# Moving a free unit of work inside the hosted groups of a fused attention and convolution block

## What is computed

```
h    = rmsnorm(concat(meta, x)) * gain                       # 272 x 2048
q, k, v, f, z_att, u, gate_b, gate_c, z_conv, m_att, m_conv = split(h @ w_in)
y_att  = (forgetting_attention(q, k, v, log_sigmoid(f + b_f)) * silu(z_att)) @ w_att_o
y_conv = (gate_b * short_conv(gate_c * u, conv_w) * silu(z_conv)) @ w_conv_o
out  = rmsnorm(x + (sigmoid(m_att) * y_att + sigmoid(m_conv) * y_conv) @ w_out) * final_gain
```

## Time and profile before

| what | value |
| --- | --- |
| median of 3 runs | 1211.78 us (1211.6 to 1213.21) |
| profiled execution, own time | 1212.1 us |
| its span, first to last instruction | 1210.4 us |
| granted TensorE clock, mean | 0.997 |
| TensorE busy | 1198.9 us, 99% |
| VectorE busy | 954.3 us, 79% |
| ScalarE busy | 651.3 us, 54% |
| the six hosted groups | 62.9 to 604.2 us of the span |

### The profile page before, as it was taken

One profiled execution on the slowest core, in us unless ns is written; L12 is line 12 of the kernel. 1 busy time (PEld: TensorE's weight loads), 2 busy tenths in 40 slices (PEclk: granted clock), 3 DMA queues, 4 the chain that ended last, 5 costly groups with the idle time before them and its releaser, 6 DMA issues.

```text
span 1210.4 us, 18441 instructions
## 1 busy us (share of the span) xinstructions
PE 1198.9 (99%) x7252; PEld 1070.5 (88%) x7252; DVE 954.3 (79%) x1111; ACT 651.3 (54%) x868; POOL 35.3 (3%) x50
## 2 busy tenths in 40 slices
PE   8999999999999999999999999999999999999997
PEld 8998898898888988889888899999999999888886
DVE  6989989989989989989966546877787778755544
ACT  7566556556556556656555444445544554543533
POOL 1000000000000000000000010111011101000000
PEclk9999999999999999999999999999999999999999
DMA  6798898897888898898678865555755565665663
GB/s 214 245 301 270 277 296 257 279 304 251 277 288 290 265 300 272 267 310 267 193 237 260 275 184 179 154 170 164 209 154 171 152 204 165 224 205 181 210 218 129
DMA packets 181249, 280.40 MB, mean 232 GB/s; under 512 B 9296, under 2 KB 128160, under 8 KB 180768
## 3 DMA queue, kind: packets, MB, share of 16 engines
q1 hardware_dynamic: 171760, 263.49, 68.1%
q10 hardware_dynamic: 9408, 15.78, 4.1%
HBM read 270.83 MB, written 8.41 MB: 231 GB/s over the span
## 4 chain that ended last, share of the span: by engine, by line
PE 89%; DVE 8%; issue 1%; ACT 1%; DMA 1%; ACTq 0%; POOLq 0%; POOL 0%; DVEq 0%
PE ps L1480 22%; PE ps L1482 22%; PE ps L1481 22%; PE ps L1494 13%; PE ps L1495 7%; DVE w_lo L1052 2%; DVE w_lo L1089 1%; DVE w_lo L1086 1%; DVE quads L1068 1%; DVE quads L1070 1%; DVE quads L1066 1%; DMA chan_rows<-in_norm_gain 1%; PE ps L1503 0%; PE ps L1527 0%; PE ps L1678 0%
## 5 line engine op out<-in xcount | busy, mean ns | idle before, releaser
L934 DVE TENSOR_TENSOR w_lo<-w_raw,w_hi 128x1024 fp32r<-128x1024 f32 x196 | 237.8, 1232 | 98.5 <-ACT w_hi L610 97.8
L1480 PE MATMUL ps<-h,w_hi 128*128 128x258 f32 (+1 forms) x1024 | 293.6, 287 | 1.2 <-DVE w_lo L1052 0.9
L1481 PE MATMUL ps<-h,w_hi 128*128 128x258 f32 (+1 forms) x1024 | 291.2, 284 | 0.0
L1482 PE MATMUL ps<-h,w_lo 128*128 128x258 f32 (+1 forms) x1024 | 290.9, 284 | 0.0
L1494 PE MATMUL ps<-h,w_hi 128*128 128x512 f32 x768 | 273.5, 398 | 0.3 <-DVE w_lo L1052 0.3
L610 ACT CAST w_hi<-w_raw 128x1024 fp32r<-128x1024 f32 x198 | 203.4, 1050 | 112.5 <-PE ps L1482 68.2
L1495 PE MATMUL ps<-h,w_lo 128*128 128x256 f32 x768 | 215.2, 280 | 0.0
L1480 PEld LDWEIGHTS ps<-h,w_hi 128*128 128x128 f32 x1024 | 192.7, 188 | 5.3 <-issue 1.8
L1481 PEld LDWEIGHTS ps<-h,w_hi 128*128 128x128 f32 x1024 | 192.9, 188 | 1.8
L1482 PEld LDWEIGHTS ps<-h,w_lo 128*128 128x128 f32 x1024 | 192.8, 188 | 0.0
L1494 PEld LDWEIGHTS ps<-h,w_hi 128*128 128x128 f32 x768 | 144.3, 188 | 35.8 <-DVE w_lo L1052 1.0
(11 more groups left out here) (209 smaller groups left out, 1836.3 us busy)
## 6 DMA issues: line engine op xcount, KB each, us to landing
w_raw<-in_w_in SPq DMA_DIRECT2D x226, 512.0 KB, 4.8
quads<-in_w_in SPq DMA_DIRECT2D x144, 512.0 KB, 4.5
w_raw<-in_w_conv_o SPq DMA_DIRECT2D x32, 512.0 KB, 5.9
w_raw<-in_w_att_o SPq DMA_DIRECT2D x32, 512.0 KB, 4.6
w_raw<-in_w_out SPq DMA_DIRECT2D x32, 512.0 KB, 4.7
quads<-in_w_in SPq DMA_DIRECT2D x48, 256.0 KB, 4.8
gates_dram<-stage ACTq DMA_DIRECT2D x24, 256.0 KB, 4.5
gate_nat<-gates_dram ACTq DMA_DIRECT2D x8, 512.0 KB, 4.5
```

What stands on the lines that cost most here:

```text
L934: nc.vector.tensor_tensor(w_lo[:, lo_slot(c), :], w_raw[:, c % RAW, :], w_hi[:, hi_slot(c), :].bitcast(F32), ALU.subtract).then_inc(w_spli ...
L1480: nc.tensor.matmul(dst, a_hi, b_hi, start=start, stop=False, skip_group_check=resumed)
L1481: nc.tensor.matmul(dst, a_hi, b_lo, start=False, stop=False, skip_group_check=resumed)
L1482: return nc.tensor.matmul(dst, a_lo, b_hi, start=False, stop=stop, skip_group_check=resumed)
```

## The change

One tuple changes. The B steps follow r = 9, 10, 11, 12, 14, 15, 16 and 17. The unit r = 13 becomes the free one in the middle of the second half, and the last B step follows r = 17, the group's last unit. The next group's step 0 follows its r = 0 as before, so that one unit instead of two lies between a group's last step and the next group's first. `B_AFTER[-1] + 2` goes from 18 to 19, which moves the second epilogue on ScalarE and VectorE by one place. `sums_after` spreads the sums of the step that now follows r = 14: two of them move to the place r = 13. Slots, quads and the loads follow from the same tuple.

```
 A_AFTER = (0, 1, 2, 3, 4, 5, 6, 7)
-B_AFTER = (9, 10, 11, 12, 13, 14, 15, 16)
+B_AFTER = (9, 10, 11, 12, 14, 15, 16, 17)
 STEP_AFTER = A_AFTER + B_AFTER
```

## The result

The changed kernel takes 1242.56 us (median, 1242.38 to 1243.07), the kernel before 1211.85 us beside it: a ratio of 1.0251, 95% interval 1.0238 to 1.0263. That is 30.7 us slower, where 22.4 were forecast. The direction was right and the time lies 2.6 us above the range.

A forecast was written before the change was run, and what follows sets the result against it. The prediction took TensorE, busy 1198.9 of 1210.4 us, as the bound. Stalls 22.4 plus one clock fall 1.7 minus relief 1.7 gave 22.4 us on 1212.1, less 0.3: 1234.2 us, range 1228 to 1240.

The forecast's parts named there:

- The bound: Whole kernel: TensorE, busy 1198.9 of 1210.4 us, sets the time; anything that makes it wait is paid in full.
- The relief: B half of each group: the free unit at r = 13 removes late VectorE splits, 1.7 us won, bounds 0 and 2.2.
- The boundary: Between groups: step 0 waits for C21 from t, the end of unit r = 0; five stalls of 3.71 to 5.04, 22.4 us.
- The clock: Behind the five boundary stalls: TensorE's clock falls to half level once, 1.7 us; bounds 0 and 8.5 us.
- three falls or more: Rival at the boundaries: the clock falls at three to five of them, 1237.6 to 1241 us; chance 0.12.
- The hidden wait: Rival at the boundaries: C21 is ready by t, so no stall, about 1210 us; chance 0.03.
- VectorE's work alone: Rival at the boundaries: the ring doesn't bind, 2.9 us stalls set by VectorE's work, 1224.6 us; chance 0.04.
- the shorter stalls: Rival at the boundaries: conv work or copies overlap better, each stall 3.7 us, about 1228.7 us; chance 0.10.
- a second lateness: Rival behind each stall: a load or cast comes late at step 1 or unit r = 2, 1239 us; chance 0.05.
- a B half without relief: Rival in the B half: the change relieves nothing there, 1.7 us more, 1235.9 us; chance within the forecast's 0.66.

The follow-up runs named there:

- e10: Changed kernel, second epilogue one place earlier (except last group), C22 two places later, step 0's first product before the C21 wait: 1210.63 us, ratio 0.9989.
- e1: Changed kernel with the second epilogue put back one place earlier on ScalarE and VectorE: 1217.41 us, ratio 1.0041.
- e2: Kernel before, with its old tuple, and only the second epilogue one place later: 1245.69 us, ratio 1.0275.
- e4: Changed kernel with the second epilogue between the two slots of step 1 on ScalarE and VectorE: 1225.65 us, ratio 1.0115.
- e9: Changed kernel with spare TensorE matmuls (40, 34, 28, 34, 40) before the C21 wait at all five boundaries: 1233.72 us, ratio 1.0174.
- e8: Changed kernel with 16 spare TensorE matmuls before the C21 wait at each of the first three boundaries: 1239.03 us, ratio 1.0214.
- e3: Changed kernel with 40, 34 and 28 spare TensorE matmuls before the C21 wait at the first three boundaries: 1238.03 us, ratio 1.0212.
- e5: Kernel before with B_AFTER = (8, 9, 10, 11, 12, 14, 15, 16), the free unit taken between A and B halves: 1253.46 us, ratio 1.0335.

## Why the prediction missed

- **The bound.** TensorE's time decides, and a wait of it is paid in full: right. The stalls and what is lost behind them add up to the longer span.
- **The relief.** Forecast at 1.7 us (1.3 in group 2 and 0.4 ahead of it), measured at 1.9 by the starts (1.4 and 0.5); e10 shows a gain of 1.6 us by the medians when nothing takes it back.
- **The boundary.** The chain (slot released at t, cast, split, conv work, copy and three operations, TensorE) came as written at four boundaries, and the five stalls are 22.6 us against 22.4. At the fifth another chain, by ScalarE's late cast, ends within 0.04 us of it, which is luck. e1 and e2 show that the cause is the epilogue's place, and e4 that without the release by the ring the third stall is 1.4 us shorter. Loads and casts behind it were hidden, as costed.
- **The clock: this step failed.** "I take one fall in five, 1.7 us": it was five in five, 9.7 us by the starts, 9.2 of them gone with the falls in e9 (8.8 by the medians). The step read the kernel's end as telling that a stall of 3.7 us was "nearer to no fall". By the same rows that fall came at 1207.2 (0.65 over 4 us is 2.8 us at half level), 4.1 us after the last matmul's start, and the one at the third boundary came just as long after t, 4.0 us. What the step left out is that the fall can still come when TensorE has begun again: there the clock fell 0.27 us after the restart, with the work of step 0 to pay for it. Nor is 4.1 us the time to a fall: at the first boundary it came 2.6 us after t. The price of one fall, 1.7 us from the earlier trace rows, was right in kind (1.6 to 2.1 at four boundaries) and short at the fifth (2.8, where half level lasts 6.8 us), so that the bound of 8.5 us for five falls was near the truth; I gave three falls or more a chance of 0.12. The Trainium skill's rule (TensorE: Matmul & The Clock Gate, HAM oscillation — how this bites in real kernels), that an idle gap between bursts of matmuls, if it is long enough, puts the clock down and can do so at every gap, was the better guide. The trace agrees at five gaps of five. Sizing the term as that sentence did, with 6.8 us more, gives 1241.0, 1.6 us from the measured time.
- **The rivals.** Three falls or more is what happened. The hidden wait, VectorE's work alone, the shorter stalls, a second lateness and a B half without relief did not.

What stays open is what brings a fall in a stretch of 1.8 to 3.2 us of idleness: e4 and e8 show it both ways. Open too is why the half level lasts 3.4 us at some boundaries and 6.8 at others.

## What to carry to other kernels

Where work is placed by counting from the last step ("two units after"), moving the step moves the work: look at what then stands in front of it, above all a slot that is released only when the waiting engine arrives. A free unit that seems idle may be the cover of an epilogue; before taking it, put the epilogue first. And price a stall of TensorE of 3.7 us or more with the clock included: here each cost its own length and 1.6 to 2.8 us behind it.

## What the runs showed of the hardware

- In the profiled executions every idle stretch of 3.7 us or more in mid-kernel (five each in the changed kernel and e2, two each in e3 and e8, six in e5) was followed by a fall of the clock. Of the five of 1.8 to 3.2 us in e4 one was, the longest; of the three of 1.9 to 3.2 us behind spare matmuls in e8 all were.
- The half level lasted 3.4 or 6.8 us. In the changed kernel a fall came 2.6 to 4.4 us after TensorE's last matmul; over all runs it came between 3.4 us before TensorE's restart (e5) and 1.1 us after it (e8).
- After a wait the first matmul of 512 columns took 0.33 us to the next start at full clock, where 0.23 is the pitch (e9).
- Spare matmuls of 240 columns through the stall kept the clock at 2.4 GHz (e3, e9). With 1.96 us of them ahead of the idleness, at stalls of 3.7 to 5.1 us, the clock fell at all three in the profiled execution of e8; shorter times suggest that it didn't at all of them in others.
